# An MLP of seven block products: the sums of weight blocks made by accumulating DMAs instead of GpSimd

## What is computed

```python
def second_block(x, ...):
    ...
        xn = rmsnorm(h, norm_mlp_g[l])
        h = h + squared_relu_mlp(xn, w_ff1[l], w_ff2[l])   # relu(xn @ w_ff1) ** 2 @ w_ff2
    return rmsnorm(h, norm_final_g)
```

## Time and profile before

| | us |
|---|---|
| median of 3 runs | 3379.59 (3378.85 to 3383.29) |
| the profiled execution | 3375.55 |
| its span, first to last instruction | 3373.8 |
| the first 512-column matmul of the MLP begins | 2696.23 |
| its last block of matmuls ends (3353.26 + 11.13) | 3364.39 |
| PE busy over the whole span | 3018.7 (89%) |

### The profile page before, as it was taken

How to read it: one execution, slowest core, us unless ns; L and a number is a source line. 1 busy time by engine, 2 the same in 40 slices (tenths; PEclk the granted TensorE clock), 3 DMA queues, 4 the chain that set the end, 5 groups by cost and what they waited for, 6 DMA issues and landing times. The chain is left out here.

```text
span 3373.8 us, 36498 instructions
## 1 busy us (share of the span) xinstructions
PE 3018.7 (89%) x14456; PEld 2254.7 (67%) x14456; DVE 1725.5 (51%) x2218; ACT 1108.4 (33%) x1640; POOL 578.7 (17%) x375
## 2 busy tenths in 40 slices
PE   7997778999998888877874999999999989999998
PEld 7886754667776575322222877888787767777776
DVE  4126856884444344111114746531215379898988
ACT  3433335663334221100003131121222354636363
POOL 0002022110000001111112000000000055656663
PEclk9998889999999999999997999999999999999999
DMA  3111000003220038999995122211113111111111
GB/s 100 47 48 6 10 14 1 1 1 119 75 81 13 26 143 344 420 421 420 415 414 235 59 67 52 81 50 50 35 55 123 38 63 51 50 51 51 50 57 50
DMA packets 140073, 370.07 MB, mean 110 GB/s; under 512 B 45888, under 2 KB 59840, under 8 KB 113920
## 3 DMA queue, kind: packets, MB, share of 16 engines
q1 hardware_dynamic: 129552, 346.97, 28.3%
q0 software_dynamic: 9216, 16.80, 1.3%
q10 hardware_dynamic: 1152, 4.19, 0.3%
HBM read 352.70 MB, written 32.83 MB: 114 GB/s over the span
## 5 line engine op out<-in xcount | busy, mean ns | idle before, releaser
L4351 PE MATMUL mlp_ps<-mlp_w_ring,mlp_a_ring 128*128 128x512 f32 x1344 | 316.3, 397 | 18.3 <-issue 13.1
L4351 PE MATMUL mlp_ps<-mlp_a_ring,mlp_w_ring 128*128 128x512 f32 x1344 | 313.1, 393 | 21.2 <-issue 13.9
L4285 POOL TENSOR_TENSOR mlp_raw<-mlp_raw 128x1024 f32<-128x1024 f32 x64 | 178.6, 2797 | 892.0 <-POOLq L572 671.0
L4351 PEld LDWEIGHTS mlp_ps<-mlp_w_ring,mlp_a_ring 128*128 128x128 f32 x1344 | 257.9, 193 | 76.1 <-issue 21.9
L4351 PEld LDWEIGHTS mlp_ps<-mlp_a_ring,mlp_w_ring 128*128 128x128 f32 x1344 | 253.0, 189 | 79.0 <-issue 24.1
L517 DVE TENSOR_TENSOR m_w_cut<-m_w_raw,m_w_cut 128x512 fp32r<-128x512 f32 (+1 forms) x86 | 80.8, 940 | 414.0 <-ACT m_w_cut L513 413.6
L2963 PE MATMUL ffn_ps<-moe_wgu,moe_rowsT 128*64 128x512 f32 x1024 | 243.0, 630 | 51.5 <-issue 25.9
L513 ACT ACTIVATE m_w_cut<-m_w_raw 128x512 fp32r<-128x512 f32 (+1 forms) x86 | 71.4, 830 | 490.4 <-PE m_gates_ps L626 190.7
L2999 DVE TENSOR_TENSOR moe_hid<-ffn_ps,moe_gated 128x256 f32<-128x256 f32 x32 | 13.6, 425 | 414.3 <-ACT moe_gated L3011 414.3
L4241 DVE TENSOR_TENSOR mlp_w_ring<-mlp_raw,mlp_w_ring 128x1024 fp32r<-128x1024 f32 x112 | 219.6, 1961 | 0.0
L2963 PEld LDWEIGHTS ffn_ps<-moe_wgu,moe_rowsT 128*64 128x64 f32 x1024 | 78.7, 145 | 195.2 <-issue 166.7
(11 more groups left out here) (575 smaller groups left out, 6457.0 us busy)
## 6 DMA issues: line engine op xcount, KB each, us to landing
moe_wgu<-in_moe_w_gate_dram SPq DMA_DIRECT2D x64, 1024.0 KB, 19.3
moe_wgu<-in_moe_w_up_dram SPq DMA_DIRECT2D x64, 1024.0 KB, 24.6
moe_wd<-in_moe_w_down_dram SPq DMA_DIRECT2D x64, 1024.0 KB, 25.5
mlp_raw<-in_w_ff_dram SPq DMA_DIRECT2D x64, 512.0 KB, 6.5
m_w_raw<-in_w_in_dram SPq DMA_DIRECT2D x48, 256.0 KB, 2.8
mix_w_raw<-in_w_in_dram SPq DMA_DIRECT2D x40, 256.0 KB, 2.6
m_w_raw<-in_w_in_dram SPq DMA_DIRECT2D x20, 512.0 KB, 3.7
x_w_raw<-in_x_w_kv_dram SPq DMA_DIRECT2D x16, 512.0 KB, 3.6
```

The source lines that it names most:

```text
L4285: nc.gpsimd.tensor_tensor(out, l, r, ALU.add if name == "S1" else ALU.subtract).then_inc(self.summed, 1)
L4351: ins = self.nc.tensor.matmul(self.ps[:, 4 * banks + tile], l, r, start=(opens and h == k == n == 0), stop=(h == k == 1 and n == 2), skip_ ...
```

## The change

The signs of the seven products are turned so that every T is a sum and no difference: T1 = B11 + B12, T2 = B22 + B11 + B12, T4 = T2 + B21, T3 = B22 + B12. To match, S1 = A21 - A22, S4 = A12 + S2, ACT takes the high part of S1 and S4 with scale -1, DVE their low part with one scalar_tensor_tensor in place of a tensor_tensor, and the products 3, 4, 5 are subtracted instead of added in `take`.

A T is no longer computed by an engine. A block is loaded by SP into a slot, and further blocks are added onto it in SBUF by DMAs with `accum_op=ALU.add`, issued by GpSimd (`load_more`, line 4218 of the changed kernel). Slot 0 holds B11, then T1; slot 1 B21; slot 2 B22, then T2 (two DMAs later), then T4 (one more); slot 3 B22, then T3. SP still issues 8 plain loads of 512 KB a unit (B22 twice, B12 never alone); GpSimd issues 10 accumulating ones a unit, 80 in all. GpSimd still makes S1, S2, S4, S3, 8 instructions a unit instead of 16. Before an accumulating DMA GpSimd waits until the slot's former content has landed (`filled`) or has been split by DVE (`w_low`). T2 of unit 0 is built inside the stage ahead (the new call `tail.gpsimd(pool)`), after a load of B22 that now goes first.

```diff
@@ project, the GpSimd program of a stage
                     side.gpsimd(pool)
+                if tail:
+                    tail.gpsimd(pool)
...
+NEGATIVE = (3, 4, 5)
+TURNED = ("S1", "S4")
+SUMS = (("S1", 0), ("S2", 0), ("S1", 1), ("S2", 1), ("S4", 0), ("S4", 1), ("S3", 0), ("S3", 1))
-SLOTS = {"B11": 0, "B21": 1, "B12": 2, "B22": 3, "T1": 0, "T2": 4, "T3": 2, "T4": 4}
+SLOTS = {"B11": (0, 1), "T1": (0, 2), "B21": (1, 1), "T2": (2, 3), "T4": (2, 4), "B22": (3, 1), "T3": (3, 2)}
+MORE = (1, 0, 3, 1)
...
+    def filled(self, eng, u, slot, h, times):
+        if times == 1:
+            eng.wait_ge(self.arrived[slot][h], 16 * (u + 1))
+        else:
+            eng.wait_ge(self.more[slot][h], 16 * (MORE[slot] * u + times - 1))
...
+    def load_more(self, pool, u, name, slot, h):
+        pool.dma_start(self.raw[:, slot, 2 * h:2 * h + 2], self.block_of(u, name, h),
+                       accum_op=ALU.add).then_inc(self.more[slot][h], 16)
...
@@ low_a
+        if name in TURNED:
+            self.nc.vector.scalar_tensor_tensor(self.a_part(g, 1).bitcast(F32R), src, -1.0, self.a_part(g, 0),
+                                                ALU.mult, ALU.subtract).then_inc(self.a_low, 1)
+            return
...
@@ take
-                nc.vector.tensor_tensor(at, ps, at, ALU.add).then_inc(self.added, 1)
+                nc.vector.tensor_tensor(at, at, ps, ALU.subtract if q in NEGATIVE else ALU.add).then_inc(
+                    self.added, 1)
...
     def begin(self, sp):
-        for name in ("B11", "B21", "B12"):
+        for name, slot in (("B22", 2), ("B11", 0), ("B21", 1)):
             for h in range(2):
-                self.load(sp, 0, name, h)
+                self.load(sp, 0, name, slot, h)
+
+    def first_sums(self, pool, u):
+        for name, times in (("B11", 1), ("B12", 2)):
+            for h in range(2):
+                self.filled(pool, u, 2, h, times)
+                self.load_more(pool, u, name, 2, h)
...
@@ run, SP for u > 0
+                        for name, slot, was in (("B21", 1, "B21"), ("B11", 0, "T1"), ("B22", 3, "T3"), ("B22", 2, "T4")):
                             for h in range(2):
+                                sp.wait_ge(self.w_low, self.split(u - 1, was, h))
+                                self.load(sp, u, name, slot, h)
...
@@ run, GpSimd
                     for u in range(len(units)):
-                        for name, h in SUMS:
+                        if u:
+                            self.first_sums(pool, u)
+                        for name, h in SUMS[:4]:
                             self.sum(pool, u, name, h)
+                            if name == "S1":
+                                pool.wait_ge(self.w_low, self.split(u, "B11", h))
+                                self.load_more(pool, u, "B12", 0, h)
+                        for name, slot, was, made in (("B21", 2, "T2", "S4"), ("B12", 3, "B22", "S3")):
+                            for h in range(2):
+                                self.sum(pool, u, made, h)
+                                pool.wait_ge(self.w_low, self.split(u, was, h))
+                                self.load_more(pool, u, name, slot, h)
```

More of the change, by code:

```diff
@@ L2524, in turned_after, with gpsimd @@
         pass
+    def gpsimd(self, pool):
+        pass
     def last_stores(self, sp):
@@ L4140, in __init__ @@
         self.arrived = [[sem(f"slot{s}_half{h}_arrived") for h in range(2)] for s in range(4)]
+        self.more = [[sem(f"slot{s}_half{h}_more") for h in range(2)] for s in range(4)]
         self.a_high, self.a_low, self.w_high, self.w_low = [sem(n) for n in ("a_high", "a_low", "w_high", "w_low")]
@@ L4215, in high_a @@
             src = self.a_sum(name, h)
-        self.nc.scalar.activation(self.a_part(g, 0).bitcast(F32R), src, ACT.Copy).then_inc(self.a_high, 1)
+        self.nc.scalar.activation(self.a_part(g, 0).bitcast(F32R), src, ACT.Copy,
+                                  scale=-1.0 if name in TURNED else 1.0).then_inc(self.a_high, 1)
     def high_w(self, act, g):
@@ L4244, in sum @@
     def sum(self, pool, u, name, h):
[L4245 to L4266, removed]
+        nc, out = self.nc, self.a_sum(name, h)
+        if name == "S1":
             self.act_ready(pool, u, "A22", h)
@@ L4300, in take @@
                         eng.wait_ge(self.added, adds + tile + 1)
-                    nc.scalar.activation(at, ps, ACT.Copy).then_inc(self.copied, 1)
+                    nc.scalar.activation(at, ps, ACT.Copy, scale=-1.0 if q in NEGATIVE else 1.0).then_inc(
+                        self.copied, 1)
                     continue
@@ L4371, in _ @@
                     for u in range(len(units)):
-                        if u:
+                        if u == 0:
+                            sp.wait_ge(rows.turned, NT)
                             for h in range(2):
-                                sp.wait_ge(self.w_low, self.split(u - 1, "T1", h))
-                                self.load(sp, u, "B11", h)
+                                self.load(sp, 0, "B22", 3, h)
+                            continue
+                        for name, slot, was in (("B21", 1, "B21"), ("B11", 0, "T1"), ("B22", 3, "T3"), ("B22", 2, "T4")):
                             for h in range(2):
-                                sp.wait_ge(self.summed, self.sum_done(u - 1, "T4", h))
-                                self.load(sp, u, "B21", h)
-                        else:
-                            sp.wait_ge(rows.turned, NT)
-                        for h in range(2):
-                            if u:
-                                sp.wait_ge(self.w_low, self.split(u - 1, "B22", h))
-                                sp.wait_ge(self.summed, self.sum_done(u - 1, "T3", h))
-                            self.load(sp, u, "B22", h)
-                        if u:
-                            for h in range(2):
-                                sp.wait_ge(self.w_low, self.split(u - 1, "T3", h))
-                                self.load(sp, u, "B12", h)
+                                sp.wait_ge(self.w_low, self.split(u - 1, was, h))
+                                self.load(sp, u, name, slot, h)
                     final.last_stores(sp, self.a_low, 14 * last)
```

34 lines of the change are left out of this document (16 added, 18 removed).

## The result

| | before | after |
|---|---|---|
| median, us | 3380.41 (3378.85 to 3383.29) | 3357.55 (3355.28 to 3357.72) |
| profiled execution / its span | 3375.55 / 3373.8 | 3357.41 / 3355.7 |
| first matmul of the stage ahead of the MLP | 2593.23 | 2602.56 |
| from there to the first of the MLP | 103.00 | 109.27 |
| first to last matmul of the MLP | 668.16 | 634.47 |

The ratio is 0.993 (95% interval 0.9913 to 0.9947): 23 us faster. 35 were forecast. The time lies inside the stated range (3334 to 3378), but not in its middle part: it falls in the band of 3353 to 3372, the second rival's "half the gain", which had 0.19, and not in 3336 to 3353, which had 0.60. The two profiles divide the difference in three: the MLP is 33.7 us shorter, the stage ahead 6.3 longer, and the stages before it, whose code is the same, end 9.3 later.

The account below looks back on a forecast made before the run. The prediction took PE's gaps, made by DVE taking turns with GpSimd, and the clock behind them as the bound: 39.9 us gained, 3.5 lost and about 1.5 for bad turns, so 35 off the median, 3344.6 us; range 3334 to 3378.

Parts of the forecast that it names:

- the second rival: In the MLP, S sums still meet low parts, or c of 2.5 to 3 takes back gain: 3362 us, chance 0.19.
- The T sums leave GpSimd: MLP: 64 sums go, DVE catches up, gaps close; 25.0 us gained in down units, 3.9 in up units.
- 0.61 and 2.54: PE gaps behind up units and ahead of the last product, in us; wait for DVE's adds behind ACT, stay.
- About 1.5 for turns that still fall badly: Loss allowed in the sum for DVE and GpSimd turns that still fall badly: about 1.5 us.
- Unit 0: MLP's first unit: gaps of 10.26, 0.14 and 0.94 become 1.8, second half late; 11.0 us gained with clock.
- Issue time c: Time GpSimd takes to issue one accumulating DMA: taken as 1.5 us, from 1.0 to 3.1 considered.
- Landing L: Time until an accumulating DMA lands: taken as 7 us, bounds 3.2 and 13.2.
- The chain of T2: Next unit's S1 waits for T2's landings, T0 - 9.3 + L + c, or squares; costs nothing within L 13.4 at c 1.5.
- T0: Time of a down unit's first matmul, from which the prediction counts the waits of T2 and the S sums.
- the first rival: GpSimd or landings bound the MLP, late at 7 unit starts; slower, priced at 3400 us, chance 0.15.
- Stage ahead: Stage before the MLP, DMA engines full: early accumulating DMAs delay its weights, 3.5 us lost, bounds 0 and 8.
- The two rules: GpSimd's DMA issues cost DVE nothing (if wrong, about 3351 us); a reducing DMA runs at half a copy's rate.

Follow-up runs that it names:

- e2: Changed kernel with T1's two accumulating DMAs moved behind the four sums S1, S2, S1, S2; 3342.98 us, ratio 0.9892.
- e1: The kernel before, run and profiled once more without any edit; 3380.2 us, ratio 0.9999.
- e8: Changed kernel with T1's DMAs behind the four sums, unit 0's held until later, and each accumulating DMA cut in two; 3340.29 us.
- e9: Changed kernel with T1's DMAs behind the four sums, unit 0's held until later, and B11 and B12 each added twice into T2; 3384.82 us.
- e3: Changed kernel with unit 0's four accumulating DMAs held until DVE has split the stage ahead's sixth weight piece; 3347.01 us, ratio 0.9895.
- e7: Changed kernel with the two DMAs behind S1 (16 of the 80) made plain, writing B12 over B11 without adding; 3349.68 us, ratio 0.9894.
- e10: Changed kernel with each of T1's two DMAs behind S2 in place of S1; 3347.72 us, ratio 0.9903.
- e4: Changed kernel without any of its 80 accumulating DMAs, the loaded block used in place of each weight sum; 3332.62 us, ratio 0.9855.

## Why the prediction was right, and where it was off

- **The T sums leave GpSimd: right.** The gaps ahead of the eighth and ninth pieces are gone, as the reading that DVE's turns with GpSimd made them says. No run puts the T sums alone back on GpSimd, so this rests on the profiles of before and after. Forecast were 25.0 us in the down units and 3.9 in the up ones. In e2, where the turns cost little, the down units give 26.5 (unit 1: 83.3 to 76.2) and the up units 5.6. The up ones were undersized because the pieces around the 0.91 us gaps were long too, 0.3 us ahead of them (5.73 for 24 matmuls) and 0.2 behind, which the prediction had set to nothing. 0.61 and 2.54 stayed, as said.
- **"About 1.5 for turns that still fall badly": the term that failed.** It is 10.6 us (changed kernel against e2), 5.2 in the down units and 5.4 in unit 0. The prediction had every turn cost one instruction of the other engine. With a DMA ahead of S2 and a sum behind it that doesn't wait for S2, a low part waits out both. That is the second rival's first condition in part, S sums that still meet low parts, at a place the prediction didn't watch: ahead of the fourth piece.
- **Two errors of opposite sign.** The gains in the MLP, as e2 shows them, are 44.3 us (42.5 against e1's profile of before) and not 39.9, and the turns took 10.6 of them and not 1.5. That the MLP as a whole missed by 4.7 only (33.7 for 38.4) is partly luck.
- **Unit 0: 11.0 forecast, 6.8 came, 12.1 in e2.** The forecast had S2's first half arrive in time and the second 1.8 us late. The gap of 4.23 is ahead of the first half, by the effect above: DVE's low part of T2 took 5.95 us. In e2 it is 0.61. The 1.8 doesn't follow from the prediction's own numbers: 6.6 for two sums and 1.5 for the DMA, less a piece of 5.45, are 2.65.
- **Issue time c, taken 1.5: 1.2.** The bounds 1.0 and 3.1 held it. Twice the rows of the indirect DMA (1.04 us) cost 1.20, much less than in proportion.
- **Landing L, taken 7: 6.2**, 8.3 at most, where the bound was 13.2.
- **The chain of T2: right that it hides.** S1 of unit 1 waited for the squares (3.81 us, released by ACT), not for a landing, and c up to 1.77 didn't lengthen the MLP (e8). In the up units, which the prediction didn't work out, S1 does stand right behind the chain (2880.44 in unit 2, T0 + 0.6), and no gap comes of it. Where it breaks, e9 is a check of the first rival: three further waits and issues after B11's first issue, 3 x (6.2 + 1.2) = 22 us, stand for L near 21. The prediction's formula then puts S1 at T0 - 9.3 + 22.2 = T0 + 12.9, and it stood at T0 + 13.7. The cost it gave for such an L was 62 us or more over seven units; 42.8 came. So the rival was a real mechanism, overpriced, and kept away by landings of 6.2 us and issues of 1.2. Its sum looked at the second half's S2 only, ahead of the sixth piece; in e9 the gap is ahead of the fifth.
- **Stage ahead: 3.5 forecast, 6.3 came** (4.9 against e1's profile of before), inside its bounds of 0 and 8; e3 shows the cause, the early DMAs. PE's wait was forecast near 6 and came to 7.6, and the clock falls with it (busy times by stretch, granted clock 0.84):

```profile
2622.00:2634.00 12.00, 4.36 (x20) 3.31 (x19) 1.23 (x1) 1.99 (x2) 2.33 (x2) 0.84 1.09 270
```

- **The base.** The profile of before had the earliest start of all. Against the median 3379.59 the forecast missed by 13 us: 4.7 in the MLP (33.7 came of 39.9 less 1.5), 2.8 in the stage ahead, and some 5.5 in the spread of the stages before, which is 9.3 by the profiles, less the 4.0 by which that profile lay under its own median.
- **The two rules.** In the changed kernel, the 43 low parts that met an issue and no sum ran at full speed (1.21 to 1.23 us). One of them, DVE, then GpSimd:

```profile
2831.20 1.21 DVE L4258 SCALAR_TENSOR_TENSOR mlp_a_ring<-mlp_sums,mlp_a_ring 128x1024 fp32r<-128x1024 f32 x1
...
2831.09 1.21 POOL L4218 DMA_DIRECT2D mlp_raw<-in_w_ff_dram  x1
```

That agrees with the Trainium skill, SBUF — State Buffer, Who interferes with whom, by which DVE with two SBUF inputs doesn't contend with a GpSimd instruction that only writes SBUF; that descriptors fall under this is inferred there. It is not the whole of what the runs show: in e8 a low part waited about 1 us beside issues, and behind an issue a second sum slipped in ahead of DVE, which was the costly part. The Trainium skill, Collectives: The Full Stack, The bandwidth ceiling, has a reducing DMA run at half a copy's rate for its two reads. e7's factor of 1.6 to 2.5 in engine time, and its 272 packets against 144, agree.

## What to carry to other kernels

Where DVE takes turns with GpSimd as here, try GpSimd's DMA issues behind a group of its sums, or let the sum that follows wait for the one before it: order alone was worth 10 us here at the same work (e2, e10). Which order is good has to be measured. A transfer started early "because its queue is idle" is not free if it lands in a stretch where another stage waits for weights; hold it on a semaphore of that stage until its last tight load is in. And compare by stage: code that did not change moved by up to 14 us between profiles here, more than half the effect that was to be measured.

## What was not expected of the hardware

- Behind a DMA issue by GpSimd, a 128x1024 tensor_tensor of DVE took 5.95 to 6.53 us, over two GpSimd sums. Without an issue none took over 3.43 (the kernel before, e4), nor over 3.67 with a second sum that waits on the first (e10). It happens with a plain DMA too (6.11, in the down units alone). Two or more issues in a row beside one sum made it 4.68 to 5.83 (e2, e8). What decides the turn stays open: only which orders show it is known.
- An accumulating DMA of 512 KB (256 rows of 2 KB) took 1.2 us to issue on GpSimd and landed in 6.2; a plain one of the same shape took 0.75 and 3.8. Half the size, adding, took 0.88 to issue.
- Stretches of the program that are the same in all kernels ended 2593 to 2607 us after the start, in twelve profiles.
